# Per-tile waits in place of all-engine barriers, and a gate chunk between the last heads of the scan

## The chip, the cores and the metric

The kernel runs on one core of one Trainium2 chip. The metric is the device time of one execution in microseconds. The kernel before took 3326.34 us (median of 3 runs, 3325.12 to 3330.06). Five engines work side by side and meet through semaphores: TensorE (PE) multiplies matrices, VectorE (DVE) and ScalarE (ACT) do elementwise work and read PSUM, GpSimd (POOL) does elementwise work in SBUF, SyncE (SP) issues the weight transfers.

## What is computed

Two blocks in sequence over 256 tokens of width 1024, all in float32. The first is one layer: three attention branches, merged through sigmoid gates, then a gated convolutional feed-forward. The second is two layers over the latent tokens and 256 context tokens: differential attention, a bidirectional state-space scan (SSD) in chunks of 128 tokens, a merge by gates, a squared-ReLU MLP. Cut to what matters here:

```python
# first block
g = sigmoid(gates.reshape(b, s, 3, D) + b_gate)
merged = g[:, :, 0] * (o_a @ w_br_a) + g[:, :, 1] * (o_b @ w_br_b) + g[:, :, 2] * (o_c @ w_br_c)
h = merged @ w_out
...
gate, val = split(conv3(h @ w_up) + conv_b)
h = (gelu(gate) * val) @ w_down
# second block, layer l
y = yf + rev(yb) + ssd_d[:, None] * xs                   # two scans over 32 heads in 8 groups
ssd = rmsnorm(y * silu(z), ssd_norm_g) @ w_ssd_o
o = (sigmoid(ga) * (att @ w_attn_o) + sigmoid(gs) * ssd) @ w_out
...
h = square(relu(h @ w1)) @ w2
```

## The kernel before

**Layout and weights.** Activations stand transposed: 128 partitions hold 128 features, the free dimension the tokens (T1 = 256 in the first block and in the last layer, TT = 512 in layer 0 of the second block, where context tokens are live too). All weights come from one stream of 315 chunks, each 128 x 8 x 256 numbers (1 MB), in the order of `chunk_order()`. SyncE loads them into a ring of four slots; it reissues a slot when TensorE has counted the chunk in it on `chunk_done`. GpSimd, ScalarE and VectorE follow the same count.

**A stage.** `pe_features` (L331 ff.) takes a chunk, waits for its PSUM pair (`take_banks`, on `evacuated`), and makes two output tiles of 128 features, each from 8 k tiles. Its argument `ready` puts a wait before each k tile of the first output tile. `pe_deep` (L373 ff.) does the same for products whose k runs over several chunks (`share` of them); it has no `ready`. PSUM pairs alternate from group to group. `evac` and `both` empty them on ScalarE and VectorE.

**Order.** Each engine's program is a straight list with its own waits. Between stages stands `bar()`, a barrier (`barrier`, L281 to L285): each of PE, ACT, DVE and POOL drains, counts up `stage_end` and waits for four counts. A barrier shows in the profile as a wait for the DRAIN of the last engine, at L284.

**Places of this case.** (1) After the 32 attention units of the first block: barrier; ScalarE applies the sigmoid to all 24 gate tiles (L1336); barrier; TensorE makes the branch products (L902), VectorE multiplies them by the gates (L1804 to L1806), GpSimd adds the three parts in place (L2232, counted on `merged`); barrier; the output projection (L348) reads the merged tiles. (2) "up" (32 chunks, L348) is convolved by VectorE, passed through gelu by ScalarE and multiplied by GpSimd (L2246, counted on `up_prod`, 16 products of two tiles each); barrier; "down" (L388) in groups of four chunks. (3) The scan of the second block: `scan_group(g)` for 8 groups of four heads. In a group TensorE turns tiles, makes the state products (L1088, L1101) and, per head, `within(r)` (L1112: 16 records at 4 token tiles, 8 at 2), and between them it projects the next group's inputs (L1050) and z (L1031), chunk by chunk. ScalarE makes each head's decay matrix (L1502, L1508), VectorE masks it (L2051); both wait for the head two before. The last group has no next group to project. Then VectorE sums (L2058) and multiplies by silu(z) (L2067); barrier; ScalarE squares Y for the norm (L1558), VectorE scales Y (L2100, counted on `z_scaled`), TensorE transposes the 16 tiles of Y (L1173) and projects the four gate chunks gs (L1165), chunk j ahead of transposes 4j to 4j+3. The transposes wait for `z_scaled`, and each for the copy out of its bank four before. (4) The last layer's MLP: mlp1 (16 chunks), squared by GpSimd (L2318); barrier; mlp2 (L388) by `pe_deep`.

A matmul of 4-byte numbers stands as two records in the trace, so a chunk at 256 columns is 32 records.

## Time and profile before

| | us |
|---|---|
| median of 3 runs (lowest, highest) | 3326.34 (3325.12, 3330.06) |
| the profiled execution | 3327.07 |
| its span, first to last instruction | 3325.3 |
| busy: TensorE, VectorE, ScalarE, GpSimd | 3120.7 (94%), 1227.8 (37%), 689.4 (21%), 538.3 (16%) |
| mean granted TensorE clock | 0.972 of 2.4 GHz |
| moved by DMA | 365.62 MB, mean 110 GB/s |

The rows further on are of four kinds. The page gives busy times and DMA issues. The waits give, by engine and line, who was waited for. The timeline gives start, length, engine, line, tiles and count of merged instructions, and in brackets the idle time before them and its releaser. The windows give each engine's busy time in a stretch, the granted clock (1.00 is 2.4 GHz, 0.50 is 1.2 GHz) and what DMA moved.

### The profile page before, as it was taken

Reading aid. Unit: us, or ns where it says so; the run is one execution under the profiler, and the core shown is the slowest. Engines: PE = TensorE matmul, PEld = TensorE weight load, DVE = VectorE, ACT = ScalarE, POOL = GpSimd, SP = SyncE. Lnnn points to the kernel's source line nnn. Section 1 sums busy time; section 2 is a strip of 40 time slices with the busy share of each in tenths; the row PEclk is TensorE's granted clock in tenths of the full one; section 3 lists DMA queues with packets and bytes.
Section 4 is the critical chain, followed back from the end, with each engine's and each line's share of the span. In section 5 each row is a group of like instructions: output and inputs, shape, how many; then the busy total and the mean of one; then the engine's idle time right before and its main releaser. Section 6 shows DMA issues by size and latency. Waiting matters only on the chain. (4 is left out here: it accounts for less than half of the span.)

```text
span 3325.3 us, 36073 instructions
## 1 busy us (share of the span) xinstructions
PE 3120.7 (94%) x14066; PEld 2394.6 (72%) x14066; DVE 1227.8 (37%) x2407; ACT 689.4 (21%) x1549; POOL 538.3 (16%) x550
## 2 busy tenths in 40 slices
PE   8998799997999899999999999998998999989998
PEld 6765688885864546666758678887876666678887
DVE  1243222204136454656523343342235555541101
ACT  1112011101013314444430020010113244440100
POOL 0000100001210002121213324442210122210100
PEclk9999899998999899999989999999999999989999
DMA  6464234341226222222212212222211322224332
GB/s 228 159 228 165 101 123 153 134 153 67 78 102 228 76 90 102 89 98 93 76 51 89 76 64 89 89 89 76 89 64 51 109 101 102 102 89 146 139 141 99
DMA packets 60827, 365.62 MB, mean 110 GB/s; under 512 B 5818, under 2 KB 17146, under 8 KB 18320
## 3 DMA queue, kind: packets, MB, share of 16 engines
q1 hardware_dynamic: 48768, 334.65, 27.9%
q10 hardware_dynamic: 10944, 25.36, 2.1%
q0 software_dynamic: 976, 3.67, 0.3%
q8 instruction: 97, 1.59, 0.2%
q14 instruction: 42, 0.34, 0.0%
HBM read 362.38 MB, written 1.28 MB: 109 GB/s over the span
## 5 line engine op out<-in xcount | busy, mean ns | idle before, releaser
L348 PE MATMUL PB<-H,ring 128*128 128x256 f32 (+1 forms) x2048 | 471.5, 394 | 26.9 <-ACT H L1387 20.7
L348 PEld LDWEIGHTS PB<-H,ring 128*128 128x128 f32 x2048 | 395.5, 194 | 102.9 <-issue 45.0
L1050 PE MATMUL PB<-H,ring 128*128 128x512 f32 (+1 forms) x1024 | 430.1, 567 | 0.0
L1050 PEld LDWEIGHTS PB<-H,ring 128*128 128x128 f32 x1024 | 192.9, 191 | 181.8 <-issue 175.6
L388 PE MATMUL PB<-work,ring 128*128 128x256 f32 x1280 | 279.7, 382 | 8.2 <-POOLq L284 7.2
L388 PEld LDWEIGHTS PB<-work,ring 128*128 128x128 f32 x1280 | 244.8, 191 | 43.0 <-issue 9.3
L1997 DVE SCALAR_TENSOR_TENSOR work<-PB,par,work 128x510 f32<-128x510 f32 (+3 forms) x256 | 182.1, 713 | 14.8 <-ACT work L1458 8.0
L1031 PE MATMUL PB<-ring,H 128*128 128x256 f32 x768 | 174.5, 382 | 4.9 <-DVE work L1997 4.9
L833 PE MATMUL PB<-H,ring 128*128 128x256 f32 (+1 forms) x640 | 177.6, 432 | 0.9 <-ACT mod L1282 0.9
L492 POOL TENSOR_TENSOR sums<-ring 128x512 f32<-128x512 f32 x53 | 68.4, 1290 | 670.9 <-PE PA L459 231.4
L348 PE MATMUL PB<-work,ring 128*128 128x256 f32 (+1 forms) x544 | 155.2, 447 | 7.7 <-POOLq L284 5.0
L1031 PEld LDWEIGHTS PB<-ring,H 128*128 128x128 f32 x768 | 143.1, 190 | 23.6 <-issue 5.7
L833 PEld LDWEIGHTS PB<-H,ring 128*128 128x128 f32 x640 | 121.1, 194 | 48.6 <-issue 35.0
L1502 ACT ACTIVATE work<-sums,work 128x128 f32<-128x128 f32 x384 | 119.0, 396 | 163.5 <-PE PA L1112 163.5
L459 PE MATMUL PB<-work,sums 128*128 128x256 f32 x680 | 150.8, 379 | 0.0
L348 PEld LDWEIGHTS PB<-work,ring 128*128 128x128 f32 x544 | 104.4, 193 | 56.9 <-issue 37.2
L459 PEld LDWEIGHTS PB<-work,sums 128*128 128x128 f32 x680 | 129.2, 190 | 17.6
L2297 POOL TENSOR_TENSOR work<-work 128x256 f32<-128x256 f32 x128 | 83.8, 679 | 289.3 <-PE PA L1112 289.3
L2281 POOL TENSOR_TENSOR work<-work 128x256 f32<-128x256 f32 x96 | 62.2, 667 | 381.8 <-ACT work L1482 312.7
L1112 PEld LDWEIGHTS PA<-work 128*128 128x128 f32 x768 | 102.2, 206 | 23.6 <-issue 11.5
L459 PE MATMUL PA<-work,sums 128*128 128x256 f32 x528 | 118.5, 379 | 0.0
L1841 DVE SCALAR_TENSOR_TENSOR work<-PB,par,work 128x254 f32<-128x254 f32 (+1 forms) x128 | 55.8, 477 | 169.0 <-ACT work L1361 164.8
(315 smaller groups left out, 4251.8 us busy)
## 6 DMA issues: line engine op xcount, KB each, us to landing
ring<-stream SPq DMA_DIRECT2D x315, 1024.0 KB, 4.8
sums<-cs_rows ACTq DMA_DIRECT2D x16, 1024.0 KB, 4.7
sums<-cs_rows ACTq DMA_DIRECT2D x16, 512.0 KB, 4.0
work<-scratch POOLq DMA_DIRECT2D x1, 2560.0 KB, 13.9
X<-xT SPq DMA_DIRECT2D x2, 1024.0 KB, 15.3
out<-H SPq DMA_DIRECT2D x1, 1024.0 KB, 4.8
con<-consts SPq DMA_DIRECT2D x1, 716.0 KB, 17.8
wdt<-w_dt POOLq DMA_DIRECT2D x1, 512.0 KB, 10.4
```

The costliest lines, as they stand in the source:

```text
L348: mm = pe.matmul(PB[:, pair, t, 0:T], ring[:, c % SLOTS, k, t * P:(t + 1) * P], rhs(k), start=(k == 0), stop=(k == KT - 1))
L388: mm = pe.matmul(PB[:, pair, t, 0:T], ring[:, c % SLOTS, k, t * P:(t + 1) * P], rhs(KT * part + k), start=(part == 0 and k == 0), stop=(pa ...
L459: mm = pe.matmul(fast_bank(side, bank)[:, col:col + T1], weight(k), right(4 * part + k), start=first and opens and k == 0, stop=last and k ...
L492: nc.gpsimd.tensor_tensor(su[:, 0], a21, a22, ALU.add).then_inc(sem("w_summed"), 1)
L833: mm = pe.matmul(PB[:, pair, t, 0:T], ring[:, c % SLOTS, k, t * P:(t + 1) * P], H[:, k, 0:T], start=(k == 0), stop=(k == KT - 1))
L1031: mm = pe.matmul(PB[:, pair, t // per, col:col + CHUNK], H[:, k, t * P:(t + 1) * P], ring[:, c % SLOTS, k, :], start=(k == 0), stop=(k == ...
L1050: mm = pe.matmul(PB[:, pair, t, 0:Tc], ring[:, c % SLOTS, k, t * P:(t + 1) * P], H[:, k, 0:Tc], start=(k == 0), stop=(k == KT - 1))
L1112: mm = pe.matmul(PA[t // 2][:, 256 * (t % 2) + HD * r:256 * (t % 2) + HD * r + HD], MB[r % 2][:, d, t, :], XC[r % 2][:, d, t, :], start=(d ...
L1502: ins = copy(MB[r % 2][:, d, t, :], BC[:, hp % 2, r % 2, d, t * P:(t + 1) * P], ACT.Relu, scale=-1.0, bias=CS[:, t, hh:hh + 1])
L1997: ins = vec.scalar_tensor_tensor(dst, src, par[:, W0 + 32 * tap + ch:W0 + 32 * tap + ch + 1], dst, ALU.mult, ALU.add)
L2281: gp.tensor_tensor(XD[d].rearrange("p (a b) -> p a b", a=4), XG[:, t, :].rearrange("p (a b) -> p a b", a=4), WD[:, t, heads].unsqueeze(2). ...
L2297: gp.tensor_tensor(XC[r % 2][:, d, :, :], XG[:, :, HD * r:HD * r + HD], DT[:, :, hh:hh + 1].broadcast_to([P, 4, HD]), ALU.mult)\
```

## The change

Barriers are taken out at the six places, and each first reader of a tile waits for the count of that tile: the branch products wait for the last attention copies (`u_out_read`, `u_read_a`); the sigmoid of the gates is cut into four pieces, each counted on `gates_open`, which VectorE waits for per branch chunk; the output projection waits for `merged` per pair of k tiles; `pe_deep` gets a `ready`, by which "down" waits for `up_prod` and mlp2 of the last layer for a new count `hid_squared`. At the scan end ScalarE waits for the last `z_used`, GpSimd for `s_fall` before its sums. A new helper `project_gs(j, t, s_)` projects a quarter of gate chunk j; in the last group the four quarters of chunk 0 stand before the four heads, and the loop over transposes projects chunks 1, 2 and 3 ahead of transposes 0, 4 and 8.

```diff
@@ -370,7 +370,7 @@
                     mm.then_inc(chunk_done, 1)
             repeat(pe, loops, body)
 
-        def pe_deep(pe, name, rhs, T, share):
+        def pe_deep(pe, name, rhs, T, share, ready=None):
 
             c0, n = CHUNKS[name][0], len(CHUNKS[name])
             per = 2 * share
@@ -385,6 +385,8 @@
                         take_banks(pe, (pair, before), it, per // share)
                     for t in range(2):
                         for k in range(KT):
+                            if ready and j < share and t == 0:
+                                ready(KT * part + k)
                             mm = pe.matmul(PB[:, pair, t, 0:T], ring[:, c % SLOTS, k, t * P:(t + 1) * P],
                                            rhs(KT * part + k), start=(part == 0 and k == 0),
                                            stop=(part == share - 1 and k == KT - 1))
@@ -886,9 +888,8 @@
                 if u >= 1:
                     values1(u - 1)
             held.finish(ada_second)
-            bar()
-            bar()
-
+            pe.wait_ge(sem("u_out_read"), len(units1))
+            pe.wait_ge(sem("u_read_a"), len(units1) - N_AB)
 
             for j in range(4):
                 c, (pair, before) = CHUNKS["branches"][j], GROUPS["branches"][j]
@@ -902,15 +903,15 @@
                             mm = pe.matmul(dst, ring[:, c % SLOTS, k, t * P:(t + 1) * P], O1[:, k, :],
                                            start=(k == k0), stop=(k == k1 - 1))
                 mm.then_inc(chunk_done, 1)
-            bar()
-            pe_features(pe, "out", lambda k: GATE[:, k, :], T1)
+            pe_features(pe, "out", lambda k: GATE[:, k, :], T1,
+                        ready=lambda k: pe.wait_ge(sem("merged"), 2 * (k // 2) + 2))
             bar()
             norm_pe(pe, "n2", T1, ONE_D)
             bar()
             norm_pe(pe, "n3", T1, ONE_D)
             pe_features(pe, "up", h1, T1, ready=lambda k: pe.wait_ge(sem("n3_h"), k + 1))
-            bar()
-            pe_deep(pe, "down", lambda k: HID1[:, k, :], T1, 4)
+            pe_deep(pe, "down", lambda k: HID1[:, k, :], T1, 4,
+                    ready=lambda k: pe.wait_ge(sem("up_prod"), k // 2 + 1))
             bar()
             norm_pe(pe, "n4", T1, ONE_D)
             bar()
@@ -1052,6 +1053,18 @@
                         if n % 4 == 3:
                             mm.then_inc(chunk_done, 1)
 
+                def project_gs(j, t, s_):
+
+                    c, (pair, before) = CHUNKS[f"gs{la}"][j], GROUPS[f"gs{la}"][j]
+                    if t == 0 and s_ == 0:
+                        take_chunk(pe, c, 0, 0)
+                        take_banks(pe, (pair, before), 0, 0)
+                    for k in range(4 * s_, 4 * s_ + 4):
+                        mm = pe.matmul(PB[:, pair, t, 0:T], ring[:, c % SLOTS, k, t * P:(t + 1) * P],
+                                       H[:, k, 0:T], start=(k == 0), stop=(k == KT - 1))
+                    if t == 1 and s_ == 1:
+                        mm.then_inc(chunk_done, 1)
+
                 def scan_group(g):
                     b = g % 2
                     tok = [t for t in range(4) if live(la, t)]
@@ -1120,6 +1133,8 @@
                     for r in range(4):
                         project(g + 1, ((5,), (6, 7), (), ())[r])
                         project_z(g, z_tiles[r])
+                        if g + 1 == SSD_GROUPS:
+                            project_gs(0, r // 2, r % 2)
                         within(r)
                     project_z(g, z_tiles[4])
 
@@ -1153,18 +1168,11 @@
                             ready=lambda k: pe.wait_ge(sem("sub_out"), LAYER["sub_out"] * la + k + 1))
                 for g in range(SSD_GROUPS):
                     scan_group(g)
-                bar()
 
                 for i in range(16):
-                    if i % 4 == 0:
-                        c, (pair, before) = CHUNKS[f"gs{la}"][i // 4], GROUPS[f"gs{la}"][i // 4]
-                        take_chunk(pe, c, 0, 0)
-                        take_banks(pe, (pair, before), 0, 0)
-                        for t in range(2):
-                            for k in range(KT):
-                                mm = pe.matmul(PB[:, pair, t, 0:T], ring[:, c % SLOTS, k, t * P:(t + 1) * P],
-                                               H[:, k, 0:T], start=(k == 0), stop=(k == KT - 1))
-                        mm.then_inc(chunk_done, 1)
+                    if i == 0 or i == 4 or i == 8:
+                        for n in range(4):
+                            project_gs(i // 4 + 1, n // 2, n % 2)
                     if i == 0:
                         pe.wait_ge(sem("z_scaled"), LAYER["z_scaled"] * la + T // P)
                     if i >= 4:
@@ -1224,8 +1232,8 @@
                     norm_pe(pe, f"m2{la}", T, ONE_D)
                     pe_features(pe, f"mlp1{la}", hl, T,
                                 ready=lambda k: pe.wait_ge(sem("mod_shifted"), past(f"m2{la}") + (k + 1) * (T // T1)))
-                    bar()
-                    pe_deep(pe, f"mlp2{la}", lambda k: HID2[:, k, 0:T], T, 4)
+                    pe_deep(pe, f"mlp2{la}", lambda k: HID2[:, k, 0:T], T, 4,
+                            ready=lambda k: pe.wait_ge(sem("hid_squared"), k // 2 + 1))
                     bar()
             norm_pe(pe, "final", T1, ONE_D)
 
@@ -1331,12 +1339,13 @@
                 if u >= 1:
                     out1(u - 1)
             held.finish(ada_second)
-            bar()
-
-            copy(GATE, GATE, ACT.Sigmoid)
-            bar()
-
-            bar()
+
+            pair, before = GROUPS["gates"][-1]
+            act.wait_ge(evacuated[pair], 2 * before + 2)
+            for j in range(4):
+                g = GATE.rearrange("p (b k) n -> p b k n", b=3)[:, :, 2 * j:2 * j + 2, :]
+                copy(g, g, ACT.Sigmoid).then_inc(sem("gates_open"), 1)
+
             evac(act, 1, "out", lambda bank, j, it: copy(HO1[:, 2 * j + 1, :], bank[:, 0:T1], ACT.Copy))
             bar()
             norm_act(act, "n2", lambda k: HO1[:, k, :], T1)
@@ -1367,7 +1376,6 @@
                             copy(UP[:, i, 0, :], UP[:, i, 0, :], ACT.Gelu_apprx_tanh).then_inc(sem("up_gelu"), 1)
             act.wait_ge(sem("n3_h"), KT)
             repeat(act, 8, up, True)
-            bar()
             evac(act, 1, "down", lambda bank, j, it: copy(one(DN1, 2 * j + 1, 2, it), bank[:, 0:T1], ACT.Copy),
                  share=4)
             bar()
@@ -1553,7 +1561,7 @@
                     if g + 1 < SSD_GROUPS:
                         silus(g + 1)
                     silu_z(g)
-                bar()
+                act.wait_ge(sem("z_used"), LAYER["z_used"] * la + 8)
                 for t in range(T // P):
                     copy(YT[:, 0:4, :], Y[:, t, :].rearrange("p (a b) -> p a b", a=4), ACT.Square,
                          accum_out=STAT[:, t:t + 1]).then_inc(sem("z_sq"), 1)
@@ -1604,7 +1612,6 @@
                 else:
                     evac(act, 1, f"mlp1{la}", lambda bank, j, it: copy(one(HID2, 2 * j + 1, 2, it)[:, 0:T],
                                                                       bank[:, 0:T], ACT.Relu))
-                    bar()
                 bar()
             norm_act(act, "final", x1, T1)
 
@@ -1794,10 +1801,9 @@
                     turned1(u - 1)
                 if u < len(units1):
                     beside(attention_fill(-1)[u], gate_out)
-            bar()
-            bar()
             for j in range(4):
                 pair, _ = GROUPS["branches"][j]
+                v.wait_ge(sem("gates_open"), j + 1)
                 v.wait_ge(chunk_done, CHUNKS["branches"][j] + 1)
                 for t in range(2):
                     k = 2 * j + t
@@ -1805,7 +1811,6 @@
                     vec.tensor_tensor(GATE[:, k, :], PB[:, pair, t, 0:T1], GATE[:, k, :], ALU.mult)
                     vec.tensor_tensor(GATE[:, 8 + k, :], PB[:, pair, t, T1:2 * T1], GATE[:, 8 + k, :], ALU.mult)\
                         .then_inc(evacuated[pair], 1)
-            bar()
             evac(v, 0, "out", lambda bank, j, it: vec.tensor_copy(HO1[:, 2 * j, :], bank[:, 0:T1]))
             bar()
 
@@ -1846,7 +1851,6 @@
                             if tap == 1:
                                 ins.then_inc(sem("up_tap"), 1)
             repeat(v, 8, up, True)
-            bar()
             evac(v, 0, "down", lambda bank, j, it: vec.tensor_copy(one(DN1, 2 * j, 2, it), bank[:, 0:T1]), share=4)
             bar()
             residual1("n4", lambda k: DN1[:, k, :], "ffn_post_g")
@@ -2092,7 +2096,6 @@
                         taps(g + 1, (r,))
                     sum_y(g)
                 times_z(SSD_GROUPS - 1)
-                bar()
                 nt = T // P
                 v.wait_ge(sem("z_root"), LAYER["z_root"] * la + 1)
                 then(vec.reciprocal(STAT[:, 8:8 + nt], STAT[:, 4:4 + nt]))
@@ -2195,7 +2198,6 @@
                     norm_mod(f"m2{la}", 4, halves)
                     evac(v, 0, f"mlp1{la}", lambda bank, j, it: vec.tensor_scalar(one(HID2, 2 * j, 2, it)[:, 0:T], bank[:, 0:T],
                                                                                 0.0, None, ALU.max))
-                    bar()
                     both(v, f"mlp2{la}", add_to(5), 4)
                     bar()
             norm_scale("final", x1, lambda k: H[:, k, 0:T1], lambda k: p_("final_g", k), T1, "h")
@@ -2220,8 +2222,6 @@
             pool.dma_start(BIAS_UP, bass.AP(scratch.tensor, 0, [[1, P], [N_REV, N_BIAS], [1, 256]]))\
                 .then_inc(sem("bias_in"), 16)
             pool.wait_ge(sem("bias_in"), 16)
-            bar()
-            bar()
             bar()
 
             for j in range(4):
@@ -2234,7 +2234,6 @@
                     pool.wait_ge(sem("merged"), 2 * j + i)
             bar()
             bar()
-            bar()
 
             c0 = CHUNKS["up"][0]
 
@@ -2246,7 +2245,6 @@
                     gp.tensor_tensor(one(HID1_PAIRS, i, 2, it), UP[:, i, 0, :], UP[:, i, 1, :], ALU.mult)\
                         .then_inc(sem("up_prod"), 1)
             repeat(pool, 8, up)
-            bar()
             bar()
             bar()
             for la in range(DEPTH_2):
@@ -2297,8 +2295,8 @@
                             gp.tensor_tensor(XC[r % 2][:, d, :, :], XG[:, :, HD * r:HD * r + HD],
                                              DT[:, :, hh:hh + 1].broadcast_to([P, 4, HD]), ALU.mult)\
                                 .then_inc(sem("s_xc"), 1)
-                bar()
                 if la == 0:
+                    pool.wait_ge(sem("s_fall"), LAYER["s_fall"])
                     pool_sums(pool, "ssd_o0")
                     pool_sums(pool, "out20")
                     bar()
@@ -2315,9 +2313,8 @@
                         pair, before = GROUPS[f"mlp1{la}"][j]
                         pool.wait_ge(evacuated[pair], 2 * before + 2 + 4 * it)
                         hh = HID2[:, span2(j, 4, it), 0:T]
-                        gp.tensor_tensor(hh, hh, hh, ALU.mult)
+                        gp.tensor_tensor(hh, hh, hh, ALU.mult).then_inc(sem("hid_squared"), 1)
                 repeat(pool, n // 4, square)
-                bar()
                 bar()
```

## Rows read from the trace of the kernel before

**Rows 1.** The page: busy time by engine; DMA issues with KB and us to landing.

```profile
PE 3120.7 (94%) x14066; PEld 2394.6 (72%) x14066; DVE 1227.8 (37%) x2407; ACT 689.4 (21%) x1549; POOL 538.3 (16%) x550
...
ring<-stream SPq DMA_DIRECT2D x315, 1024.0 KB, 4.8
```

**Rows 2.** Waits of TensorE: line <- releaser: us in total, times, longest.

```profile
PE PA L756 <- DMA par<-params: 9.9, 1, 9.9
PE PB L388 <- POOLq L284: 7.2, 2, 5.0
```

**Rows 3.** Timeline (start, us, what, idle before), gates of the first block.

```profile
328.84 0.27 ACT L1323 ACTIVATE work<-PA 64x128 f32<-64x128 f32 x1 [3.60 <-PE PA L873]
329.23 5.32 ACT L1336 ACTIVATE work<-work 128x6144 f32<-128x6144 f32 x1
...
334.62 5.49 PE L902 MATMUL PB<-work,ring 128*128 128x256 f32 x12 [5.82 <-ACTq L284]
```

**Rows 4.** Timeline, from the branch products to the output projection.

```profile
367.48 2.60 POOL L2232 TENSOR_TENSOR work<-work 128x512 f32<-128x512 f32 x2 [4.29 <-DVE work L1806]
...
370.20 11.97 PE L348 MATMUL PB<-work,ring 128*128 128x256 f32 x45 [4.99 <-POOLq L284]
```

**Rows 5.** Timeline, from "up" to the first down projection.

```profile
635.71 11.39 PE L348 MATMUL PB<-H,ring 128*128 128x256 f32 x52
...
650.49 1.26 POOL L2246 TENSOR_TENSOR work<-work 128x512 f32 x1 [12.53 <-DVE work L1841]
652.14 18.03 PE L388 MATMUL PB<-work,ring 128*128 128x256 f32 x70 [5.05 <-POOLq L284]
```

**Rows 6.** Timeline, start of the last layer's mlp2.

```profile
3198.17 20.12 PE L388 MATMUL PB<-work,ring 128*128 128x256 f32 x92 [2.19 <-POOLq L284]
```

**Rows 7.** Windows: stretch, length, busy by engine, PEclk, DMA share, GB/s.

```profile
334.60:340.00 5.40, 5.38 (x13) 4.30 (x14) 0.00 (x0) 0.00 (x0) 0.00 (x0) 0.50 0.00 0
370.20:376.00 5.80, 5.79 (x18) 4.78 (x19) 0.00 (x0) 0.00 (x0) 0.00 (x0) 0.65 0.00 0
652.10:658.00 5.90, 5.86 (x15) 4.68 (x16) 0.00 (x0) 0.00 (x0) 0.00 (x0) 0.54 0.00 0
970.50:975.00 4.50, 4.26 (x25) 1.55 (x26) 3.96 (x9) 1.45 (x4) 0.00 (x0) 0.62 0.22 71
3198.10:3204.00 5.90, 5.83 (x27) 5.17 (x28) 0.00 (x0) 0.00 (x0) 0.00 (x0) 1.00 0.36 150
```

**Rows 8.** Timeline, scan of layer 0: a middle group's head, then the end.

```profile
1557.91 1.90 PE L1112 MATMUL PA<-work 128*128 128x64 f32 x16
1559.64 7.09 PE L1050 MATMUL PB<-H,ring 128*128 128x512 f32 x16
...
1665.93 5.26 PE L1112 MATMUL PA<-work 128*128 128x64 f32 x32 [3.02 <-issue]
...
1672.77 7.09 PE L1112 MATMUL PA<-work 128*128 128x64 f32 x32 [1.58 <-DVE work L2051]
...
1682.55 16.89 PE L1165 MATMUL PB<-H,ring 128*128 128x512 f32 x32 [2.69 <-DVEq L284]
...
1692.56 4.88 DVE L2100 TENSOR_SCALAR work<-work,small 128x2048 f32<-128x2048 f32 x4
...
1701.02 13.90 PE L1165 MATMUL PB<-H,ring 128*128 128x512 f32 x32
```

**Rows 9.** Timeline, scan end of layer 1, and one window of it.

```profile
2948.84 1.28 ACT L1502 ACTIVATE work<-sums,work 128x128 f32<-128x128 f32 x4 [14.74 <-PE PA L1112]
...
2951.70 3.68 PE L1112 MATMUL PA<-work 128*128 128x64 f32 x16 [1.25 <-DVE work L2051]
...
2956.94 9.44 PE L1165 MATMUL PB<-H,ring 128*128 128x256 f32 x32 [1.56 <-DVEq L284]
...
2962.86 2.48 DVE L2100 TENSOR_SCALAR work<-work,small 128x2048 f32<-128x2048 f32 x2
...
2945.00:2950.00 5.00, 3.19 (x15) 3.22 (x16) 2.34 (x7) 1.16 (x4) 1.17 (x2) 0.50 0.00 0
```

## The prediction

> **What bounds the kernel now.** I read the page first: TensorE is busy 3120.7 us of the span of 3325.3 and no other engine reaches 40% [rows 1], so time can be won only where TensorE stands still, or runs at the lower of its two clock levels. Then the waits of TensorE by releaser [rows 2]: a line that names L284 is a barrier, and what stands before the arrow is the work that was held. Only one wait of TensorE is for a transfer, 9.9 us at the start. A chunk of weights lands 4.8 us after its issue [rows 1] and feeds TensorE for 6.9 us (32 records at 256 columns; each matmul is two records) or 13.8 us (at 512), so the ring has slack. Third, the timeline around each place that the change touches [rows 3 to 6, 8, 9], and last the granted clock behind each stop [rows 7]. What a stretch at 1.2 GHz costs is its length times the share of clock that is missing.
>
> **Gates.** Now: ScalarE's last copy of the attention ends at 329.11, the sigmoid over all 24 tiles takes 5.32, and the branch products start at 334.62 [rows 3]. After: they wait for that copy alone and start at 329.2, 5.4 us earlier. The sigmoid is four pieces of about 1.5 us, which end near 335.3; VectorE asks for the first only when a branch chunk is done, after 336, so it is hidden. The first 5.4 us of the branches run at 1.2 GHz now and lose 2.7 [rows 7]. The clock had already fallen during the thin last units of the attention, so the new start is slow too; dense work begins sooner after the fall, and I take 0.5 back. Sum 5.9, bounds 5.0 and 7.0.
>
> **Output projection.** TensorE ends the branches at 365.22, GpSimd the merging at 370.08, and the projection starts at 370.20 [rows 4]. After: its k tiles 0 to 5 need merges that are ready, 12 records or 2.6 us; then it waits for the last merge, as late as now. So 2.6 of the 5.0 us gap is filled and 2.4 stay. The row that decides the clock is the gap of 2.19 before the second down projection [rows 6], behind which the clock stayed at 2.4 GHz (1.00) [rows 7]; behind the present 5.0 it is 0.65 over 5.8 us, a loss of 2.0. I give the loss back: 4.6, bounds 2.6 and 4.7.
>
> **First down projection.** TensorE ends "up" at 647.10, GpSimd's last product is ready at 651.75, and the down projection starts at 652.14 [rows 5]. After: the first group's first chunk needs only products 1 to 4 of 16, long there; product 16 is wanted in the fourth chunk, 20 us later. The PSUM pair it takes is that of up chunk 30, which VectorE reads while TensorE computes chunk 31. So the gap of 5.05 goes, and with it the 2.7 us of half clock behind it (5.9 us at 0.54) [rows 7]. The added waits are satisfied and stand in TensorE's queue ahead of matmuls; those of "up" have the same form and its chunks keep their 6.9 us [rows 5]. Minus 0.2 for the loop's entry: 7.6, bounds 5.0 and 7.8.
>
> **Second down projection.** The same with a gap of 2.19 [rows 6] and no loss of clock: 2.1.
>
> **Scan end, layer 0.** Now: last state product ends at 1662.9, then four heads with waits between them end at 1679.86, VectorE sums and multiplies by z, the barrier opens and gate chunk 0 runs 1682.55 to 1699.4, 16.9 us instead of 13.9 at 1.2 GHz for its first part; the transposes wait for VectorE's scaling, done at 1697.44, and for that chunk, and start at 1699.3 [rows 8]. So from the end of the last head to the scaled Y are 17.6 us. After: chunk 0 is cut into four pieces of 3.44, one ahead of each head. (A chunk takes 13.75, or 13.9 with the run-out of its last record; a head at 2.4 GHz 1.90, or 1.73 to the start of the next work [rows 8].) Head 0 waits for VectorE until 1665.9 anyway, so piece 0 costs it nothing. Heads 2 and 3 need ScalarE's exponentials, which it starts when head 0 or 1 is done: head 2 now starts at 1672.77, 4.9 after head 0 (1665.93 + 1.90), and pieces 1 and 2 with head 1 take 8.6. TensorE's own work then sets the end: 1662.75 + 13.75 + 4 x 1.73 = 1683.4, 3.5 later than now, and scaled Y stands at 1701.1. Behind the heads chunk 1 runs to 1697.2 and leaves a new idle stretch of 3.9 us: that wait replaces the barrier. The transposes start at 1701.2, 1.9 later than now (1699.3), with one chunk (13.75) less behind them: 11.85. Two deductions. The nearest gap, 3.85 us before L996, was followed by 0.62 of the clock over 4.5 us, a loss of 1.7 [rows 7]. And the last eight transposes now follow each other with no chunk between; their copies out of PSUM (0.7 each, two engines, and a gate's two sigmoids of 0.54) hold them 0.7 us longer. Sum 9.5, bounds 7.8 and 11.2. GpSimd's wait for the decay reads is over by 1677; its sums need chunk ssd_o0, which SP issues when chunk 0 is done: earlier than now.
>
> A rule speaks against this part. By the Trainium skill ("TensorE: Matmul & The Clock Gate", section "HAM oscillation — how this bites in real kernels"), bursts of matmuls with waits between them keep the clock falling back again and again. The trace agrees as far as it goes: both scan ends run at half clock through such bursts [rows 8, 9]. By the rule the gain is smaller by the half clock behind the new 3.9 us, which the sum takes from a row; left out, the sum would be 1.7 higher.
>
> **Scan end, layer 1.** Half the tokens: chunk 6.9, piece 1.72. Here the heads end at 2955.38 and scaled Y stands at 2965.34, 9.96 later [rows 9]. The clock falls at 2944.5, owed to gaps ahead of the heads that do not change, so piece 0 takes 3.4 us to 2947.7; head 0 follows until 2948.6, as now. ScalarE starts for head 2 at 2948.84 and head 2 follows at 2951.70, 2.9 us later; behind pieces 1, 2 and head 1 it would start at 2952.9, so it does not wait. The last head ends at 2956.4, chunk 1 at 2963.3, scaled Y at 2966.4, against transposes at 2966.1 now, behind chunk 0 (2966.38 with its run-out). So 6.9 - 0.3 = 6.6; minus half of 1.7 for the clock behind 3.1 us of idle time (between the 2.19 that cost nothing and the 3.85 that did), minus 0.3 for the end: 5.5, bounds 4.0 and 7.3.
>
> **Sum.** 5.9 + 4.6 + 7.6 + 2.1 + 9.5 + 5.5 = 35.2. The profiled execution took 3327.07 (span 3325.3), 0.7 above the median of three, 3326.34: 3327.07 - 35.2 - 0.7 = 3291.2, given as 3291. The bounds add up to 26.4 and 40.5, or 3300.0 and 3285.9. Everything behind each place starts from TensorE's last product, so what TensorE gains is passed on whole.
>
> **Rivals.** (a) The clock gives nothing back: the three refunds (0.5, 2.0, 2.7) fail, sum 30.0, 3296. For it: the clock fell at both scan ends behind gaps of only 2 to 3 us. Against: 2.19 cost nothing [rows 7]. (b) The pieces lengthen the head chain instead of filling it. In layer 0 the four pieces would push the last head to 1679.9 + 13.75 = 1693.6 and the transposes to 1711.2, leaving 13.75 - 11.9 = 1.9 before deductions; in layer 1, 2962.3 + 10.0 against 2966.1 leaves 0.7. Then the sum is 35.2 - 7.6 - 4.8 = 22.8, 3303.6. Against: the heads stand still for 3.0 and 1.6 us now and at half clock besides [rows 8]. (c) The waits bind as the barriers did (a tile needed early is produced last, as in the output projection): only 20 us or less, 3307. Against: the products' order in "up" is their order of use. (d) Slower: the barriers gave the weights' ring time to refill, and without them TensorE waits for each chunk. The place is the 56 chunks at 256 columns from the branches to the first down projection. It decides from a landing time of 6.9 us: to end 0.2% slower than before, 42 us must be lost, 0.75 per chunk, so 7.65 us per landing; at 8.0 it is 62 lost, 3353. Against: 4.8 us, and no wait for a transfer in steady work [rows 1, 2].
>
> **Chances.** Forecast as worked out (3286 to 3299) 0.68; (a) 0.13; (b) 0.10; (c) 0.06; (d) 0.02; something that eats all but 6.6 us 0.01. The range reaches from the upper bound of the gains, with 2 us for the spread of runs, to between (a) and (b): 3284 to 3302; left out are (b), (c), (d). About 0.2%, 6.6 us, is what a measurement of this kernel can tell from no change: faster by more 0.95, within 0.03, slower 0.02.
>
> **What would show it.** TensorE's waits on L284 before L902, L348, L388 and L1165 are gone. The branch products start 0.1 us behind the last copy; the output projection stops once for about 2.4 us behind 12 records; no gap ahead of L388 in either down projection. In each scan's last group, records of the new helper lie between the heads, at 1.00 of the clock in layer 0; VectorE's scaling releases the first transposes after an idle stretch of 3 to 4 us. The forecast is wrong if that stretch is over 6 us, if L388 waits for GpSimd at its start, or if waits on the ring appear.

## The result and the profile after

| | before | after |
|---|---|---|
| median of the first four runs | 3327.21 | 3291.49 |
| the profiled execution, its span | 3327.07, 3325.3 | 3291.58, 3289.8 |
| TensorE busy | 3120.7 | 3109.1 |
| mean granted clock | 0.972 | 0.976 |

The ratio is 0.9892, 95% interval 0.9875 to 0.9909; the forecast was 3291.0 in a range of 3284 to 3302. A second set of four executions of the changed kernel, with a second profile (e10), gave 3291.38. The pages show what kind of gain it is: TensorE does the same 14066 records; it stands still 24 us less (span less busy time, 204.6 and 180.7) and is busy 12 us less, because it runs at 1.2 GHz for a shorter time.

The waits of TensorE after (line <- releaser: us in total, times, longest). The barriers before the branches and both down projections, and in front of the gate chunks, are gone; the wait of 7.2 for L284 in [rows 2] has no line any more. Three new waits stand in their place, the third of 0.4 us:

```profile
PE PS L1181 <- DVE work L2103: 6.7, 2, 3.7
...
PE PB L348 <- POOL work L2232: 2.4, 1, 2.4
...
PE PB L903 <- ACT work L1331: 0.4, 1, 0.4
```

(L1181 are the transposes, L2103 is VectorE's scaling of Y; L2232 is GpSimd's merge.) The timeline of the first block after, against [rows 3 to 5]:

```profile
326.96 0.27 ACT L1331 ACTIVATE work<-PA 64x128 f32<-64x128 f32 x1 [3.34 <-PE PA L875]
327.25 5.60 ACT L1347 ACTIVATE work<-work 128x1536 f32<-128x1536 f32 x4
327.28 5.22 PE L903 MATMUL PB<-work,ring 128*128 128x256 f32 x12 [0.36 <-ACT work L1331]
...
357.38 2.75 PE L348 MATMUL PB<-work,ring 128*128 128x256 f32 x12
...
359.88 2.60 POOL L2232 TENSOR_TENSOR work<-work 128x512 f32<-128x512 f32 x2 [4.30 <-DVE work L1812]
362.53 9.72 PE L348 MATMUL PB<-work,ring 128*128 128x256 f32 x36 [2.40 <-POOL work L2232]
...
624.79 8.37 PE L348 MATMUL PB<-H,ring 128*128 128x256 f32 x38
...
632.99 7.29 PE L390 MATMUL PB<-work,ring 128*128 128x256 f32 x33
```

The branches start 0.05 us behind the last copy (326.96 + 0.27), with the four sigmoids beside them. The output projection does its 12 records and then stands for exactly 2.40 us. L390, the first down projection, has no idle time in brackets: it follows "up" record to record. The windows behind these places, the answer to [rows 7] (PEclk, the granted clock, is the third number from the end):

```profile
327.30:332.70 5.40, 5.40 (x14) 4.33 (x15) 0.00 (x0) 5.40 (x4) 0.00 (x0) 0.55 0.00 0
362.50:368.30 5.80, 5.77 (x19) 4.75 (x20) 0.00 (x0) 0.00 (x0) 0.00 (x0) 0.71 0.00 0
633.00:639.00 6.00, 6.00 (x29) 5.30 (x28) 1.75 (x4) 1.02 (x2) 1.26 (x1) 1.00 0.49 175
1681.70:1688.20 6.50, 6.45 (x21) 4.85 (x22) 1.50 (x2) 2.35 (x4) 4.99 (x4) 0.58 0.10 39
```

The scan end of layer 0 after, against [rows 8]: four pieces of chunk 0 (L1063) between the heads (L1125), at full clock; then chunk 1, and the idle stretch.

```profile
1643.25 3.60 PE L1063 MATMUL PB<-H,ring 128*128 128x512 f32 x8
...
1646.69 1.89 PE L1125 MATMUL PA<-work 128*128 128x64 f32 x16
1648.42 3.65 PE L1063 MATMUL PB<-H,ring 128*128 128x512 f32 x8
...
1662.35 1.89 PE L1125 MATMUL PA<-work 128*128 128x64 f32 x16
1664.08 13.95 PE L1063 MATMUL PB<-H,ring 128*128 128x512 f32 x32
...
1676.82 4.87 DVE L2103 TENSOR_SCALAR work<-work,small 128x2048 f32<-128x2048 f32 x4
...
1681.75 1.97 PE L1181 MATMUL PS<-con,work 128*128 128x128 f32 x8 [3.72 <-DVE work L2103]
```

The same end in layer 1, the last head, chunk 1 and the transposes:

```profile
2926.95 1.00 PE L1125 MATMUL PA<-work 128*128 128x64 f32 x8
...
2927.79 7.13 PE L1063 MATMUL PB<-H,ring 128*128 128x256 f32 x32
...
2937.86 0.66 PE L1181 MATMUL PS<-con,work 128*128 128x128 f32 x4 [2.94 <-DVE work L2103]
```

**By place.** I took the start of each stage's first TensorE record in both timelines. The lead is how much earlier that record starts after the change; by how much the lead grows from one stage to the next is what the stage gave.

| place | forecast (bounds) | measured |
|---|---|---|
| gates, to the end of the branches | 5.9 (5.0 to 7.0) | 6.0 |
| output projection | 4.6 (2.6 to 4.7) | 2.9 |
| first down projection | 7.6 (5.0 to 7.8) | 7.8 |
| second down projection | 2.1 | 2.35 |
| scan end, layer 0 | 9.5 (7.8 to 11.2) | 8.7 |
| scan end, layer 1 | 5.5 (4.0 to 7.3) | 6.4 |
| sum of the six | 35.2 | 34.1 |
| all other stages together | 0 | 1.4 |

The last line is small but not quiet: the start gave 1.9, the entry of "up" 3.1, the first attention of the second block took 3.7, the final norm 1.7, all with the same instructions. (Here and below, this attention's 104.1 or 107.8 us are counted from the fifteenth of its 32 units to the first projection of the scan.) The experiments come back to it.

### The profile page after: what moved, and what is told of

It reads as the page before. It is cut to its first block, busy times and chain, and to the rows that moved or that the text cites. A ratio compares the mean times of both kernels' runs of the same rounds, so it can differ in the third digit from the quotient of the medians.

```text
span 3289.8 us, 36064 instructions
## 1 busy us (share of the span) xinstructions
PE 3109.1 (95%) x14066; PEld 2387.6 (73%) x14066; DVE 1226.6 (37%) x2407; ACT 690.7 (21%) x1552; POOL 535.1 (16%) x550
## 4 chain that ended last, share of the span: by engine, by line
PE 67%; DVE 7%; ACT 2%; issue 1%; DVEq 0%; POOLq 0%; POOL 0%; ACTq 0%
PE PB L1051 11%; PE PB L461 9%; PE PB L348 9%; PE PA L461 6%; PE PB L390 5%; PE PS L461 4%; PE PB L1032 4%; PE PB L949 3%; PE PB L835 3%; DVE work L2001 2%; PE PA L1125 2%; PE PB L1063 2%; PE PA L1101 1%; PE PA L557 1%; PE PA L1114 1%
## 5 line engine op out<-in xcount | busy, mean ns | idle before, releaser
L390 PE MATMUL PB<-work,ring 128*128 128x256 f32 x1280 | 276.9, 379 | 1.2 <-ACT work L1578 1.2
L390 PEld LDWEIGHTS PB<-work,ring 128*128 128x128 f32 x1280 | 243.1, 190 | 34.5 <-issue 1.4
L1032 PE MATMUL PB<-ring,H 128*128 128x256 f32 x768 | 174.5, 382 | 5.0 <-DVE work L2001 5.0
L949 PE MATMUL PB<-ring,H 128*128 128x256 f32 x512 | 115.7, 379 | 0.0
## 6 DMA issues: line engine op xcount, KB each, us to landing
work<-scratch POOLq DMA_DIRECT2D x1, 2560.0 KB, 13.9
wdt<-w_dt POOLq DMA_DIRECT2D x1, 512.0 KB, 10.5
```

The source lines that it names most:

```text
L390: mm = pe.matmul(PB[:, pair, t, 0:T], ring[:, c % SLOTS, k, t * P:(t + 1) * P], rhs(KT * part + k), start=(part == 0 and k == 0), stop=(pa ...
L949: mm = pe.matmul(PB[:, pair, t // 2, CHUNK * (t % 2):CHUNK * (t % 2 + 1)], H[:, k, t * P:(t + 1) * P], ring[:, c % SLOTS, k, :], start=(k ...
L1032: mm = pe.matmul(PB[:, pair, t // per, col:col + CHUNK], H[:, k, t * P:(t + 1) * P], ring[:, c % SLOTS, k, :], start=(k == 0), stop=(k == ...
```

## Experiments

Each edit is on the changed kernel unless it says otherwise. "Local" is the length of the stage in the two timelines; the median holds everything. The changed kernel's medians were 3291.49 and 3291.38; I compare with 3291.4. The kernel before had medians of 3327.18 in the rounds of e1 to e4, 3327.05 in those of e5 to e8 and 3325.60 in those of e9 to e12, so medians of different rounds can differ by 1.5 us without an edit.

**e1: the pieces undone, no barriers.**

```diff
-                        if g + 1 == SSD_GROUPS:
-                            project_gs(0, r // 2, r % 2)
...
-                    if i == 0 or i == 4 or i == 8:
+                    if i % 4 == 0:
                         for n in range(4):
-                            project_gs(i // 4 + 1, n // 2, n % 2)
+                            project_gs(i // 4, n // 2, n % 2)
```

> The changed kernel, but gate chunk 0 stands whole behind the heads again and chunks 1 to 3 ahead of transposes 4, 8 and 12; all barriers stay out. Theory (the pieces fill standing time of the heads, and scaled Y, not TensorE, opens the transposes): layer 0, last head at about 1660.4, scaled Y and the transposes at about 1678, 3.7 us earlier than with the pieces, but 13.75 us more behind them: 10 us slower there, less some 3 for the clock and the tail; layer 1, 6.9 - 1 = 6 slower. In all 12 to 14 us slower than the changed kernel, 3304 to 3306. Rival (the pieces only lengthen the heads, the barrier's removal is the gain): at most 3 us slower, 3291 to 3295.

Measured 3302.41, 11.0 slower than the changed kernel (ratio to before 0.9928, 0.9914 to 0.9941), a little less than the 12 to 14 expected. Local: 8.5 slower in layer 0, 5.5 in layer 1, together the upper end of it; stages that the edit does not touch gave some back, the final norm 1.7. So against the kernel before, taking the barrier out alone gave 0.2 us in layer 0 (497.4 against 497.6 from the first of the scan's turns, L1080, to the first record of its output projection) and 0.9 in layer 1. The timeline of e1 shows why:

```profile
1646.64 7.06 PE L1125 MATMUL PA<-work 128*128 128x64 f32 x32 [3.02 <-issue]
1655.16 7.09 PE L1125 MATMUL PA<-work 128*128 128x64 f32 x32 [1.46 <-DVE work L2053]
1662.04 16.39 PE L1063 MATMUL PB<-H,ring 128*128 128x512 f32 x32
1674.83 4.88 DVE L2101 TENSOR_SCALAR work<-work,small 128x2048 f32<-128x2048 f32 x4
1679.76 1.09 PE L1179 MATMUL PS<-con,work 128*128 128x128 f32 x8 [1.33 <-DVE work L2101]
```

Chunk 0 follows the heads without a stop, but the heads and the first part of the chunk run at half clock (16.39 us, where [rows 8] has 16.89 and a chunk at full clock 13.9), and the transposes wait for scaled Y, 17.5 us after the last head as ever. The rival (the pieces only lengthen the heads) is out.

**e2: the pieces kept, the barrier back at both scan ends** (a `bar()` on each of the four engines behind the last group).

> The changed kernel with the pieces kept, and the barrier at both scan ends put back. Theory (scaled Y opens the transposes, 17.6 us after the last head, and chunk 1 takes only 13.9 of them): the barrier delays chunk 1 by 2.7 us, which comes out of the 3.7 us that TensorE stands still before the transposes; the transposes start no later. 0 to 1 us slower in time, or up to 3 faster if the shorter idle stretch keeps the clock up: 3289 to 3293. Rival (the barrier costs what its wait shows, 2.7 and 1.6 us): 3295 to 3296.

Measured 3285.47, 5.9 faster than without these barriers. That is more than the theory allowed. Locally layer 0 was 1.05 faster, layer 1 0.3 slower:

```profile
1669.20 16.65 PE L1063 MATMUL PB<-H,ring 128*128 128x512 f32 x32 [2.69 <-DVEq L284]
...
1679.26 4.88 DVE L2106 TENSOR_SCALAR work<-work,small 128x2048 f32<-128x2048 f32 x4
...
1685.70 1.04 PE L1182 MATMUL PS<-con,work 128*128 128x128 f32 x8
```

TensorE now stands still ahead of chunk 1, 2.69 us for the barrier, and not behind it, 3.72 us. The chunk then runs partly at 1.2 GHz (16.65), the transposes start 1.6 us behind scaled Y, but at full clock, and nothing stands idle. So the barrier at the scan end costs nothing once the pieces are there; the rival (4 us) is out. The other 5 us of the median are not at the scan ends; the profiled execution took 3291.13 and the three others 3285.24 to 3285.51. Its trace says this much: against the first profile of the changed kernel it was 5.2 us longer from TensorE's first record to the first branch product (322.5 against 317.3, with 6.8 us at 1.2 GHz in the program's start against none) and shorter in the attention of the second block and in the final norm. That the three faster executions were spared the long start would account for them, but they have no trace.

**e3: the two barriers before the branches back.**

> The changed kernel with the two barriers before the branch products put back (the sigmoid stays cut into four pieces). Theory: TensorE starts the branches 5.7 us later (the whole sigmoid ends first), and the end of the branches moves by 6.0 with the clock: 3297.5. Rival (the earlier start is lost to the clock or to VectorE's wait for the gates): under 2 us, 3291.5 to 3293.5.

Measured 3298.13, 6.7 slower. The branches start behind the fourth sigmoid (337.83, [6.12 <-ACTq L284]), and their first 5.4 us run at 0.52 of the clock, with the early start at 0.55: the clock is a small part of this place, as forecast. Local, as the start of the first block's norm against that of e2, whose program start lay within 0.3 us of this one: 6.0.

**e4: the barrier before the first down projection back.**

> The changed kernel with the barrier before the first down projection put back. Theory: a gap of 5.05 us and 2 to 3 us of half clock behind it, 7.0 to 8.0 us slower: 3299. Rival (the clock behind the gap is no cost of the barrier, it falls anyway): 5.0 us, 3296.5.

Measured 3295.21, 3.8 slower: below both expectations. But local the place cost 7.6, inside the theory's 7.0 to 8.0, made up of the gap and a slow start:

```profile
636.90 1.26 POOL L2248 TENSOR_TENSOR work<-work 128x512 f32 x1 [12.54 <-DVE work L1848]
638.67 6.53 PE L390 MATMUL PB<-work,ring 128*128 128x256 f32 x19 [5.16 <-POOLq L284]
...
638.70:644.60 5.90, 5.90 (x17) 4.83 (x18) 0.00 (x0) 0.00 (x0) 0.00 (x0) 0.63 0.00 0
```

(The last line is a window.) The difference came back in the attention of the second block (104.0 instead of 107.8 in this profile), far from the edit. The five executions ran from 3293.59, the profiled one, to 3298.15.

**e5: the barrier before the output projection back.**

> The changed kernel with the barrier between the branch products and the output projection put back. In the trace of the changed kernel 12 records stand ahead of the wait and the gap fell from 4.99 to 2.40, but the clock fell behind it all the same. Theory (only the filled 2.6 us and a little clock were won): 2.6 to 3.3 us slower, 3294.5. Rival (my forecast of the place, with the clock refunded): 4.6, 3296.

Measured 3295.65, 4.2 slower. Local, from the branches to the norm, 2.65: the theory. The rest is the entry of "up" (224.0 instead of 221.1 for the stage), so the median alone would have spoken for the rival.

**e6: the first output chunk makes k tiles 0 to 5 of both its output tiles first.**

```diff
-            pe_features(pe, "out", ...)
+                for ks in ((range(6), (6, 7)) if j == 0 else (range(KT),)):
+                    for t in range(2):
+                        for k in ks:
```

> The changed kernel, but the output projection's first chunk makes k tiles 0 to 5 of both its output tiles before k tiles 6 and 7 of either: 12 more records (2.6 us) ahead of the wait for the last merge, which stands for 2.40 us now. Theory (the remaining gap and the half clock behind it are the cost of the order, not of the waits): the gap goes and 1.7 us of clock with it, 3.5 to 4.5 us faster than the changed kernel, 3287.5. Rival (the clock falls in any case, owed to what went before): 2.4 faster, 3289.

Measured 3291.03, 0.4 faster: nothing that counts. Yet the place did what was expected, 4.5 us local: 24 records now cover the merge, TensorE has no gap, and the clock stays up. Most of it, 2.9 us, was taken again at the entry of "up". The three windows are e6 at the output projection, e6 at "up", and the changed kernel at "up":

```profile
356.60:362.40 5.80, 5.80 (x28) 4.97 (x27) 2.08 (x6) 0.00 (x0) 2.52 (x2) 1.00 0.50 181
407.20:415.00 7.80, 7.80 (x23) 6.40 (x24) 2.60 (x7) 0.00 (x0) 0.00 (x0) 0.62 0.00 0
```

```profile
411.90:419.70 7.80, 7.79 (x36) 6.89 (x37) 2.63 (x7) 0.55 (x2) 0.00 (x0) 1.00 0.01 2
```

The norm ahead of "up" is the same in both, with 21 us of mostly idle TensorE. In the changed kernel the clock has come back when "up" begins, in e6 it has fallen once more.

**e7: the idle stretch before the transposes filled.** ScalarE opens gate chunk 0 directly behind the last head, where it stood idle, so its PSUM pair is free for the first part of chunk 2.

```diff
+                    ahead = 1 if la == 0 else 2
                     if i == 0 or i == 4 or i == 8:
-                        for n in range(4):
+                        for n in range(ahead if i == 4 else 0, 4):
                             project_gs(i // 4 + 1, n // 2, n % 2)
+                    if i == 0:
+                        for n in range(ahead):
+                            project_gs(2, n // 2, n % 2)
...
+                act.wait_ge(sem("s_within"), LAYER["s_within"] * (la + 1))
+                open_gs(0)
                 act.wait_ge(sem("z_used"), LAYER["z_used"] * la + 8)
```

> The changed kernel, and the idle stretch before the first transposes filled: ScalarE opens gate chunk 0 as soon as the last head is done (it stands idle then), which frees its PSUM pair, and TensorE projects the first quarter (layer 0) or half (layer 1) of chunk 2 ahead of the wait for scaled Y. Theory (the 3.72 and 2.94 us of standing still are real room, and the half clock behind the first is owed to it): layer 0 3.4 us and 2 to 3 us of clock, layer 1 2.9 less 0.5: 7 to 9 us faster than the changed kernel, 3283.5. Rival (the sigmoids ahead of the squares delay scaled Y by as much, a table load of 1.28 and 1.1 us each): 3 us faster or less, 3289.

Measured 3278.43, 13.0 faster than the changed kernel (ratio to before 0.9851, 0.9837 to 0.9864). Local 6.1 in layer 0 and 3.8 in layer 1, 9.9 together, a little above the 7 to 9 of the theory; the attention took the shorter time too (104.1). The other 3 us of the median lie outside the edit's own places.

```profile
1666.12 17.39 PE L1063 MATMUL PB<-H,ring 128*128 128x512 f32 x40
...
1666.33 1.09 ACT L1572 ACTIVATE work<-PB 128x512 f32<-128x512 f32 x2 [0.40 <-PE PA L1125]
...
1668.91 1.91 ACT L1578 ACTIVATE work<-work 128x2048 f32<-128x2048 f32 x1 [1.50 <-DVE work L2081]
...
1683.80 1.09 PE L1185 MATMUL PS<-con,work 128*128 128x128 f32 x8 [0.29 <-DVE work L2113]
```

Five quarters of a chunk run through, and 0.29 us of standing still are left of 3.72. The sigmoids end before ScalarE's squares can begin, so they delay nothing: scaled Y still comes 17.5 us after the last head.

**e8: e6 and e7 together.**

> The new order of the output projection's first chunk and the filled scan ends together. Both places lie far apart and TensorE is the bound in between, so their gains add: 11 to 13 us faster than the changed kernel, 3279 to 3281. If they do not add, the fall of the clock elsewhere has taken a part.

Measured 3280.93: in the expected range of times, 10.5 faster than the changed kernel where 11 to 13 was written, but 2.5 slower than e7 alone. Local the gains are all there (4.5, 6.1, 3.2); the entry of "up" took 3.0 back, the attention took 108.0.

**e9: the barriers back at all six places, only the pieces left.**

> The changed kernel with all barriers back in their six places, so that only the pieces of gate chunk 0 between the last heads are left of the change (and the waits per tile, which are then satisfied). Theory: the pieces give 8.5 and 5.5 us at the two scan ends, less at most 1 for the barriers there: 13 us faster than the kernel before, 3313 to 3315; together with the 18.5 of the four other barriers the whole change. Rival (the pieces gain only when the barrier is gone too): 3320 or more.

Measured 3311.04, 14.6 faster than the kernel before, 3325.60 in these rounds (ratio 0.9956, 0.9942 to 0.9969). Local 9.7 and 6.1. So the change splits into about 15 us for the pieces, which need no barrier to go, and about 19 for the five other barriers, four in the first block and one in the last MLP (6.0 + 2.9 + 7.8 + 2.35). The last of these, before the second down projection, has no run of its own; in e9's trace its stage is 2.5 us longer than in the changed kernel's. The expected gain was 13; that the barriers at the scan ends cost nothing (e2) accounts for up to 1 of the 1.6 above it. The rival (no gain from the pieces while the barrier stands) is out.

**e10: the changed kernel again.**

> The changed kernel once more, for a second profile. In the traces so far the stretch of the first attention of the second block (32 units) with the same instructions lasted 104.1 us in four kernels, with 24 us of it at 1.2 GHz, and 107.8 in the others, with 37; the start 14.1 or 16.0. Theory (where the clock falls in stretches of thin work depends on how the execution happens to lie, not on the kernel): the second profile may show the other value, and the times spread over 3 us or more: 3287 to 3293. Rival (each kernel has its own value): the same 107.8, and times within 1.5 us of 3291.5.

Measured 3291.38, from 3289.45 to 3292.72. The second profile of one and the same kernel holds the other value for the first attention of the second block. The first window is from the first profile, the second from e10:

```profile
1033.60:1141.30 107.70, 95.66 (x502) 58.06 (x495) 50.14 (x137) 35.51 (x104) 3.16 (x3) 0.83 0.33 120
```

```profile
1035.70:1139.80 104.10, 89.72 (x502) 54.83 (x495) 49.39 (x137) 34.60 (x103) 3.16 (x3) 0.89 0.34 125
```

502 matmul records in each, 3.6 us apart, with 37.5 and 23.9 us at 1.2 GHz. The start went the other way (14.1 and 16.0). The rival (each kernel has its own value) is out.

**e11: e7, and the modulation's 24 chunks spread over all 32 attention units.**

```diff
-            + ([(f"ada{la + 1}", u)] if la == 0 and u < ADA_CHUNKS else []) for u in range(units)]
+            + ([(f"ada{la + 1}", u - (u + 2) // 4)] if la == 0 and u % 4 != 2 else []) for u in range(units)]
```

> The kernel with the filled scan ends (e7), and the 24 chunks of the next layer's modulation that are worked off beside the attention units lie in three of every four of all 32 units instead of in the first 24. The last eight units, where TensorE stood still 1.4 us in each and the clock fell for 24 to 37 us, get work, the others fewer. Theory (the fall is owed to those thin units): the attention stretch drops to 101 to 104 and the time is 1 to 4 us faster than with the filled scan ends alone, 3275 to 3278. Rival (the units are bound by the chain of softmax and transposes, and units without a chunk are no shorter for it): no difference, or up to 2 us slower.

Measured 3283.98, 5.6 slower than e7. The theory fell, and the rival (at most 2 us slower) does not cover it either: the attention, here counted from its second modulation chunk to the scan's first projection, took 192.7 us in this profile, e7's 189.2. The times were 3278.24 to 3286.08.

**e12: e11 with e6.**

> The same with the new order in the output projection too. It was 4.5 us faster up to the first block's norm and lost 2.9 again in the up projection, where its clock was still at 1.2 GHz for 6 us. Theory (that give-back belongs to the position of the norm and comes again): 1.5 us faster than e11. Rival (it was chance): 4.5 us faster than e11.

Measured 3277.65 (ratio 0.986, 0.9845 to 0.9875), 6.3 faster than e11, more than either expectation, with three runs within 0.15 us of 3277.6 and one at 3284.59. The same stretch took 185.5 with 5.5 us at 1.2 GHz, against 23.9 in e11, with the same work; 6.6 us of the difference lie in one product of 64 records behind the attention (7.36 against 13.92 us). Between e12 and e7 (3278.43, 3274.52 to 3279.71) the runs do not decide; both beat the kernel before by 1.4 to 1.5% and the changed one by 0.4%.

## Why the prediction was right, and where it was not

**Gates.** Right in mechanism and size: 6.0 for 5.9, and e3 gives it back (6.0 local). 5.5 us of it are the earlier start behind the last copy; the clock gave 0.3 (the lead was 7.3 when the branches began and 7.7 when they ended), where I had 0.5.

**Output projection.** The step that failed is the refund, the half clock behind a gap that I took back together with the gap. I wrote that behind the remaining 2.4 us the clock would stay up, because it had behind 2.19 [rows 6, 7]. It fell: 0.71 of the clock over 5.8 us behind the 2.40 gap, against 0.65 before. So this term was 2.9 and not 4.6, with the 2.6 for the twelve records right (the gap fell from 4.99 to 2.40). It was no accident of one profile: in all seven other profiles with this gap the projection took the same 33.3 us to the norm. One row of a gap that cost nothing was too little ground: the length of a gap alone does not decide here, since 2.97 us at the program's start cost nothing in the first profile and 3.4 us of half clock in e10. e6 shows that the mechanism was understood: without the gap the place gave 4.5.

**First down projection.** Right: 7.8 for 7.6, gap 5.05 and 2.8 of clock; the 0.2 for the loop's entry was not there. Here the refund came, since no gap is left at all. **Second:** 2.35 for 2.1; 2.19 of it is the gap, and here too I had taken a little off for the loop's entry that was not there.

**Scan ends.** The chain was forecast to within 0.4 us: with the lead of 19.5 us taken off, the last head should end at 1663.9 and ended at 1664.24, the transposes at 1681.7 and 1681.75; the idle stretch was to be 3.9 and was 3.72. The 9.5 became 8.7 because the clock behind that stretch cost more than the 1.7 I took from the nearest gap: 0.58 over 6.5 us, 2.7. The wait that takes the barrier's place was the right picture, and e7, which fills it, is the best proof. In layer 1 the chain came as forecast too: with the lead of 28.5 taken off, the last head was due to end at 2927.9 and ended at 2927.95, the transposes at 2937.9 and 2937.86. The 5.5 became 6.4 because the deductions were too large: the clock did not fall behind the 2.94 (1.00 over the next 6.2 us), where I had taken off 0.85. What the forecast did not say, and e1, e2 and e9 show: here the pieces are the whole gain and taking the barrier out is worth 0.2 and 0.9 us alone, and -1.05 and 0.3 beside the pieces.

**The rivals.** (a), no refund, was true of the output projection (0.3 of 2.0 came back) and not of the first down projection (2.8 for 2.7); at the gates 0.3 of 0.5 came. (b) is out by e1 and e9. (c) happened at the output projection alone, as written in its own step. (d) is out: a chunk still lands before TensorE wants it, and no wait for the ring appeared.

**The rest.** That the sum met the time to 0.5 us is partly luck. The six places were 1.1 short of the forecast and the untouched stages gave 1.4, the net of shifts of up to 3.7 us in both directions. The bounds as written add up to 26.5 and 40.1, not 26.4 and 40.5; the range does not change by it.

## What to carry to other kernels

When a barrier goes, ask which chain opens the next stage: where it is the one that ran behind the barrier too (here the norm of Y, 17.5 us), only work moved into that chain's standing time gains, and the barrier's own wait is no measure. Behind a wait per tile, order the consumer so that what needs the last tile comes last for all its outputs; in e6 that filled the 2.4 us which the new wait had left. Judge an edit of a few microseconds by the length of its own stage in the trace beside the median, because the clock moves other stages by as much.

## What the runs showed of the hardware

The same instructions took different times in thin stretches of TensorE work, where it stops again and again, by whether the clock had fallen in them: the later part of the attention 104.1 or 107.8 us, in two profiles of one kernel too; "up" 221.1 or 224.0 by what its norm left; the program's start 14.1 or 16.0, with none or 3.4 us of it at 1.2 GHz. I found no single longer gap that goes with the slower case. So a gain of 4.5 us (e6) could vanish from the median and one of 9.9 appear as 13.0 (e7). Whether an execution's place is chance or set by the kernel's timing these runs do not settle: e12 and e2 had three executions within 0.3 us and one 5.7 to 7 above, e4 was spread over 4.6 and e5 over 5.2.

The Trainium skill ("TensorE: Matmul & The Clock Gate", section "HAM oscillation — how this bites in real kernels") describes bursts of matmuls with waits between them that keep the clock falling. The traces agree, with shorter waits than in the page's example: at the end of layer 0's scan the clock stayed at 1.2 GHz for 20.5 us before, with no gap over 3.02 us there [rows 8], for 6.8 after, and for none in e7.
